# Seven extra weight tiles instead of four, expert rows gathered from x, and first units multiplied kind by kind in a two-block fp32 kernel on one core

## The chip, the cores and the metric

The kernel runs on one core of a Trainium2 chip as a single launch. The metric is device time in microseconds (us), here the median of three runs of the kernel before: 1743.42 us (1740.96 to 1744.84). All inputs and weights are fp32 in HBM and have to be fetched once: the trace counts 548 MB, of which the experts of two mixture layers are 403 MB.

## The reference, cut to what matters

One sequence of 256 tokens with 1024 features goes through a first block of two layers and then a second block. What the change touches, in the reference's own functions:

```
def modulate(x, g, shift, scale):                 # before every mixer and every expert layer
    return rmsnorm(x, g) * (1 + scale) + shift

def ec_moe(h, w_router, w_gate, w_up, w_down):    # 16 experts, each takes its best 32 tokens
    cap = 2 * n // 16
    aff = softmax(h @ w_router);  g, idx = top_k(aff.swapaxes(1, 2), cap)
    xs = h[idx]
    a = silu(xs @ w_gate) * (xs @ w_up)
    y = (a @ w_down) * g;  return zeros.at[idx].add(y)

layer 0:  x += g_m * even_mixer(modulate(x));  x += g_f * ec_moe(modulate(x))   # attention and Fourier
layer 1:  x += g_m * odd_mixer(modulate(x));   x += g_f * ec_moe(modulate(x))   # gated short convolution
second_block: mLSTM and attention in parallel, cross attention to mem, then relu^2 feed-forward
```

A row's RMS factor is a scalar per token. It can therefore be applied to the row, to the one-hot matrix that picks the row, or inside the matrix that transposes it; the result is the same up to rounding.

## The kernel before

Everything is written by hand: five engine programs (TensorE, VectorE, ScalarE, GpSimd, SyncE) joined by semaphores, with no scheduler. The order of each engine's instructions is the order of its Python code, and an engine that waits holds up everything behind it.

**The ring.** Weights come in units of 1 MB (128 partitions x 2048 fp32), listed by `weight_units` and issued in that order by SyncE alone. They go to `ring`, 12 slots (`SLOTS`); outside the expert layers only 8 of these (`TAIL`) are in the rotation, since the other 4 hold the two parts, `hi` and `lo`, of units that are multiplied in split form. `room(g)` in SyncE's program waits until the unit that sat in the slot has been read.

**An expert layer.** An expert has 12 units: 4 of gate, 4 of up, 4 of down. `pe_moe` computes router logits (`lgp`, `lgn`), VectorE makes softmax, top 32 and the one-hot matrices `take_p` (tokens x places), and `expert(e)` then runs 16 times: gather 32 rows by one-hot matmul (L727), transpose, gate and up (L742), silu and product, down (L765), and scatter into four PSUM banks (L774). After each unit TensorE raises `MOE_READ`, which lets SyncE refill the slot. The first two experts are unrolled. Expert 0's units fill the 12 ring slots; the first 4 units of expert 1 go to `extra` tiles, 1 MB stretches of SBUF that are idle just then (scratch at 42, 0 and 8 KB, and `hT`). So 16 units can be there when expert 0 begins; `left` and `turn_of` name for each extra tile what SyncE waits for and where in its order the load stands.

**Rows for the experts.** ScalarE squares x, VectorE makes the factor, and both scale x into `xn` (`norm_rows`, `scaled`); the gather reads `xn`.

**Split products.** The layer-1 mixer (`CONV_ORDER`, 16 units), the attention input (`in0`) and the feed-forward (`FF_ORDER`) multiply fp32 as three fp32r products: hi x hi, hi x lo, lo x hi. ScalarE casts a unit to `hi` (`round_weights`, L2015), VectorE subtracts to `lo` (`rest_of_weights`, L1466), and the three products are taken together for each k (L636, L651, L530), so the first product of a stage waits for both parts of both operands.

**The joints.** From layer 0's experts to the mixer: add the four banks to x, squares, factor, scale rows to `xn`, 16 transposes (L495), scale and shift (`turned`), cast and subtract for the rows, then unit 0. From layer 1's experts to the second block: VectorE first norms the rows of `mem` (L1224) and only then adds the banks to x (L1437), after which x is transposed (L503) for `in2.0` (L544).

## Time and profile before

| | |
|---|---|
| median of 3 runs | 1743.42 us (1740.96 to 1744.84) |
| the profiled execution, its own time | 1744.17 us |
| its span, first to last instruction | 1742.3 us |
| mean granted TensorE clock | 0.877 of full |
| TensorE busy | 1347.6 us, 77% |
| VectorE, ScalarE busy | 545.5 us, 348.4 us |
| moved by DMA | 548.10 MB, mean 315 GB/s |

The profiled execution lies 0.75 us above the median, and 1.9 us of it are outside the span. The page's 40 slices are 43.6 us each. Two long stretches at 421 to 422 GB/s are the expert layers (slices 8 to 16 and 21 to 30); between and behind them the traffic is much lower and TensorE is near fully busy. An instruction's line (L742) is its line in the kernel. A timeline row gives start, length, engine, line, tiles and count, and in brackets how long the engine had been idle and who released it; consecutive rows of one group are merged, so a length can span several instructions. An fp32 matmul has two records in the trace, a transpose or an fp32r product has one.

### The profile page before, as it was taken

The numbers are of one execution on the slowest core, as the hardware profiler recorded it, in microseconds if no ns is written. First come the engines' busy times: TensorE is split into PE (matmuls) and PEld (weight loads), VectorE is DVE, ScalarE is ACT, GpSimd is POOL, SyncE is SP. The second block draws the span as 40 slices with busy tenths as digits, with TensorE's granted clock in tenths as the row PEclk, the third lists the DMA queues.
The fourth block names the chain that finished last, engine by engine and source line by source line (L and its number), as shares of the span: only waits on it lengthen the run. The fifth ranks groups of instructions, "written<-read, shape, count | busy, mean of one in ns | idle before, by whom it ended". The sixth has DMA issues, their size and how long they took to land. (4 is left out here: it accounts for less than half of the span.)

```text
span 1742.3 us, 29625 instructions
## 1 busy us (share of the span) xinstructions
PE 1347.6 (77%) x12416; PEld 903.6 (52%) x12416; DVE 545.5 (31%) x1168; ACT 348.4 (20%) x610; POOL 27.9 (2%) x54
## 2 busy tenths in 40 slices
PE   3999996765665667599676667667668979989998
PEld 1997583322222223299442233233337856778997
DVE  2576753101010100256411010000103266555554
ACT  2413421000000000243300000000002132254443
POOL 2010100000000000000000000000000000000000
PEclk8999997889789887899798787887879997999999
DMA  9986898999999999965699999999998420345550
GB/s 329 361 293 236 282 361 345 420 422 421 422 422 422 422 421 421 389 210 172 269 420 421 422 422 421 422 422 422 422 421 265 139 85 12 114 150 176 192 167 25
DMA packets 145053, 548.10 MB, mean 315 GB/s; under 512 B 9630, under 2 KB 77632, under 8 KB 95704
## 3 DMA queue, kind: packets, MB, share of 16 engines
q1 hardware_dynamic: 142336, 542.18, 79.3%
q10 hardware_dynamic: 1080, 4.16, 0.7%
q0 software_dynamic: 1568, 0.77, 0.4%
q8 instruction: 51, 0.84, 0.2%
q14 instruction: 18, 0.15, 0.0%
HBM read 546.03 MB, written 1.05 MB: 314 GB/s over the span
## 5 line engine op out<-in xcount | busy, mean ns | idle before, releaser
L742 PE MATMUL bank<-ring,scratch 128*32 128x256 f32 x3968 | 311.4, 462 | 161.5 <-DMA ring<-in_moe_w_up 112.4
L742 PEld LDWEIGHTS bank<-ring,scratch 128*32 128x32 f32 x3968 | 134.7, 127 | 322.6 <-DMA ring<-in_moe_w_up 173.4
L765 PE MATMUL bank<-ring,scratch 128*32 128x256 f32 x2048 | 161.5, 463 | 60.7 <-DMA ring<-in_moe_w_down 44.8
L636 PE MATMUL bank<-scratch_split,ring_split 128*128 128x256 f32 x1344 | 161.2, 281 | 7.8 <-DVE scratch_split L1584 5.8
L636 PEld LDWEIGHTS bank<-scratch_split,ring_split 128*128 128x128 f32 x1344 | 160.1, 192 | 9.6 <-issue 6.0
L1418 DVE COPY scratch<-bank 128x256 f32<-128x256 f32 x32 | 13.6, 424 | 452.1 <-PE bank L751 452.1
L765 PEld LDWEIGHTS bank<-ring,scratch 128*32 128x32 f32 x2048 | 68.3, 130 | 147.2 <-DMA ring<-in_moe_w_down 74.2
L1466 DVE TENSOR_TENSOR ring_split<-ring,ring_split 128x2048 fp32r<-128x2048 f32 x48 | 110.0, 2292 | 76.8 <-ACT ring_split L2015 76.7
L516 PE MATMUL bank<-ring,hT 128*128 128x256 f32 (+1 forms) x512 | 112.8, 381 | 1.3 <-DVE hT L1233 0.7
L1997 ACT ACTIVATE scratch<-bank 128x256 f32<-128x256 f32 x32 | 12.3, 384 | 503.7 <-PE bank L742 503.7
L516 PEld LDWEIGHTS bank<-ring,hT 128*128 128x128 f32 x512 | 97.2, 193 | 14.6 <-issue 2.1
L2015 ACT CAST ring_split<-ring 128x2048 fp32r<-128x2048 f32 x48 | 91.3, 1904 | 57.3 <-PE bank L1145 36.8
L530 PE MATMUL bank<-ring_split 128*128 128x256 f32 x512 | 94.3, 288 | 9.2 <-DVE ring_split L1458 9.2
L1145 PE MATMUL bank<-ring_split,scratch_split 128*128 128x512 f32 x384 | 90.7, 392 | 0.5 <-DVE scratch_split L1897 0.5
L1425 DVE TENSOR_TENSOR scratch<-bank,gate 128x256 f32<-128x256 f32 x32 | 13.6, 424 | 245.7 <-PE bank L765 245.7
L530 PEld LDWEIGHTS bank<-ring_split 128*128 128x128 f32 x512 | 80.0, 193 | 12.0 <-DVE ring_split L1458 9.6
L1145 PEld LDWEIGHTS bank<-ring_split,scratch_split 128*128 128x128 f32 x384 | 70.9, 188 | 15.5 <-issue 1.1
L1993 ACT COPY scratch<-bank 128x256 f32<-128x256 f32 x32 | 11.9, 373 | 305.9 <-PE bank L727 305.9
L559 PE MATMUL bank<-ring,cond 128*32 128x256 f32 x768 | 50.9, 403 | 14.5 <-DMA ring<-in_ada_w 14.5
L774 PE MATMUL bank<-scratch 32*128 32x256 f32 x512 | 42.2, 447 | 20.4 <-DVE scratch L1425 20.4
L1397 DVE TENSOR_TENSOR scratch<-bank,gain 128x128 f32<-128x128 f32 x64 | 15.6, 286 | 106.0 <-PE bank L732 106.0
L774 PEld LDWEIGHTS bank<-scratch 32*128 32x128 f32 x512 | 27.7, 206 | 36.1 <-issue 35.7
(418 smaller groups left out, 1416.2 us busy)
## 6 DMA issues: line engine op xcount, KB each, us to landing
ring<-in_moe_w_up SPq DMA_DIRECT2D x128, 1024.0 KB, 26.7
ring<-in_moe_w_down SPq DMA_DIRECT2D x128, 1024.0 KB, 26.5
ring<-in_moe_w_gate SPq DMA_DIRECT2D x120, 1024.0 KB, 25.4
ring<-in_ada_w SPq DMA_DIRECT2D x48, 1024.0 KB, 8.8
ring<-in_w_ff SPq DMA_DIRECT2D x32, 1024.0 KB, 5.3
ring<-in_conv_w_in SPq DMA_DIRECT2D x12, 1024.0 KB, 11.9
ring<-in_attn_w_in SPq DMA_DIRECT2D x10, 1024.0 KB, 11.8
ring<-in_w_in SPq DMA_DIRECT2D x7, 1024.0 KB, 11.9
```

Of the source, the lines that this page charges most:

```text
L516: mm = nc.tensor.matmul(T[:, t * 256:t * 256 + width], lhs[:, k, t * P:(t + 1) * P], W[:, k, :], start=(k == ks[0]), stop=(k == ks[-1]))
L530: mm = nc.tensor.matmul(T[:, t * 256:t * 256 + 256], ht[:, k, t * P:(t + 1) * P], wt[:, k, :], start=(k + i == 0), stop=(k == KD - 1 and i ...
L559: mm = nc.tensor.matmul(T[32 * j:32 * j + 32, c0:c0 + 256], cond[:, k, :], W[:, a, j * 256:j * 256 + 256], start=(k == 0), stop=(k == 7))
L636: mm = nc.tensor.matmul(T[:, m * SEQ:(m + 1) * SEQ], wt[:, k, m * P:(m + 1) * P], ht[:, k, :], start=(k + i == 0), stop=(k == KD - 1 and i ...
L742: mm = nc.tensor.matmul(GU[32 * j:32 * j + 32, m * 256:(m + 1) * 256], xs[:, k % 2, 16 * k - k % 2 * 16:16 * k - k % 2 * 16 + 32], W[:, (k ...
L765: mm = nc.tensor.matmul(Y[32 * g:32 * g + 32, 0:256], actT[:, b, 32 * j:32 * j + 32], W[:, b * D + g * 256:b * D + (g + 1) * 256], start=( ...
L774: mm = nc.tensor.matmul(banks[4 + g][:, t * 256:(t + 1) * 256], comb[32 * g:32 * g + 32, t * P:(t + 1) * P], y_s[32 * g:32 * g + 32, :], s ...
L1145: mm = nc.tensor.matmul(acc[2 * t + c][:, :], ht[:, u % 2, a, t * P:(t + 1) * P], wt[:, a, c * 512:(c + 1) * 512], start=(u + a + i == 0), ...
L1397: ins = V.tensor_tensor(own, T[:, b * P:(b + 1) * P].rearrange("p (g c) -> p g c", g=4), bc(gain[:, l, 2, b::2].unsqueeze(2), [P, 4, CAP]) ...
L1418: V.tensor_copy(comb, banks[1][:, 256:512]).then_inc(comb_ready, 1)
L1466: give("w_split", V.tensor_tensor(lo[n % 2], ring[:, q, :], hi[n % 2], ALU.subtract))
L2015: sig("w_hi").give(A.copy(w_parts[p][0][n % 2], ring[:, q, :]))
```

## The change

- `EXTRA` = 7 extra tiles take the first 7 units of expert 1, and `TURN` = 5 is now the number of ring slots whose refill belongs to expert 1. The new tiles are `table_tile` (the constants that aren't needed then), `rows_tile` (`xn`) and `upper` (scratch at 34 KB). The constant table is put in another order for it, small buffers of the expert layer move, and `mask_q` is loaded a second time behind `mem`.
- The gather reads x itself. The row factor (`row_scale`) is multiplied into `take_p`, and `aff` is multiplied by its inverse so that the scatter weights stay as they were.
- The layer-1 rows are transposed by a matmul with `diag`, the identity times the row factor, in place of scaled rows and transposes; ScalarE writes the `hi` part straight from PSUM. `pe_gate(1, 2)` moves from the joint to behind the fourth conv unit.
- The first unit of each split stage (`pe_in0_first`, `pe_split_first`) is multiplied kind by kind: all hi x hi, then the weights' lo, then the rows' lo.
- At the start SyncE no longer waits for two small loads, and unit `in0.0` is cast before the rows. The norm of `mem` moves behind the rotary angles. The output is stored in four parts of 256 KB.

```diff
-for _name, _n in (("ident", 128), ("rank", CAP), ("cos", 128), ("sin", 128), ...
+for _name, _n in (("ident", 128), ("rank", CAP), ("inv_freq", 32), ("fold", 16), ("spread", 128), ("mask_k", 512),
+                  ("pick", 512), ("pick_ada", 512), ("mask_q", 512), ("dft_cos", 512), ("dft_sin", 512),
+                  ("grp_cos", 128), ("grp_nsin", 128), ("cos", 128), ("sin", 128)):
...
-        extra = [[high, low, turned_tile, mid], [high, mid, low, turned_tile]]
+        turned_tile, rows_tile = carve(HT, 0, UNIT), carve(XN, 0, UNIT)
+        table_tile = carve(TB, TABLE["mask_q"][0] / 256.0, UNIT)
+        extra = [[table_tile, high, low, turned_tile, rows_tile, mid, upper],
+                 [table_tile, high, upper, mid, low, rows_tile, turned_tile]]
...
-        base = [(TAIL + TAIL * l) % SLOTS for l in range(3)]
+        base = [(TAIL + TURN * l) % SLOTS for l in range(3)]
...
-            if isinstance(e, int) and e == 1 and s < 4:
+            if isinstance(e, int) and e == 1 and s < EXTRA:
                 return extra[l][s], extra_landed[s], 16 * (l + 1)
-            i = s if isinstance(e, int) and e == 0 else (s + TAIL) % SLOTS
+            i = s if isinstance(e, int) and e == 0 else (s + TURN) % SLOTS
...
+        def pe_split_first(pe, p, name, h, bank):
+            ...
+            sig("w_hi").take(pe, (1, len(CONV_ORDER))[p])
+            for b in range(4):
+                sig(("h1_hi", "h4_hi")[p]).take(pe)
+                run(hi, h[0], (2 * b, 2 * b + 1), first=True)
+            pe_split_unit(pe, p, 0)
+            run(lo, h[0], range(KD))
+            for b in range(4):
+                sig(("h_split", "h4_split")[p]).take(pe)
+                mm = run(hi, h[1], (2 * b, 2 * b + 1), last=True)
...
-                                              xn[:, t, g * 256:(g + 1) * 256], start=(t == 0), stop=(t == 1))
+                                              x[:, t, g * 256:(g + 1) * 256], start=(t == 0), stop=(t == 1))
...
-            pe_gate(pe, 1, 2)
             pe_ada_cols(pe, 1, 1)
-            pe_turn_rows_after(pe, "n1")
+            sig("diag_ready").take(pe)
+            for b in range(4):
+                T = tile(pe, f"n1.{b}")
+                for i in range(4):
+                    k = 2 * b + i // 2
+                    mm = nc.tensor.matmul(T[:, i * P:(i + 1) * P], x[:, i % 2, k * P:(k + 1) * P], diag[:, i % 2, :],
+                                          start=True, stop=True)
+                done(f"n1.{b}", mm)
             for n, (part, u) in enumerate(CONV_ORDER):
                 if n == 4:
+                    pe_gate(pe, 1, 2)
                     pe_router_bias(pe, 1)
...
+                        step(ins)
+                    own = take_p[:, :, e:e + n, :].rearrange("p t e c -> p t (e c)")
+                    return V.tensor_tensor(own, own, bc(row_scale.unsqueeze(2), [P, 2, n * CAP]), ALU.mult)
...
-                if l == 1:
-                    v.wait_ge(loads["mem"], 16)
-                    norm_rows(mem_raw, mem_n, ss_ctx)
-
                 for b in range(4):
                     v.wait_ge(combined, 4 * (e0 + NEXP - 1) + b + 1)
...
-            norm_rows(x, xn, ss, 2)
+            sig("squares_ready").take(v)
+            step(V.tensor_reduce(ss[:, 0:2], pieces[:, :, 0:2], AX, ALU.add))
+            rms(ss, [(0, 2, D)])
+            for t in range(TT):
+                ins = V.tensor_scalar(diag[:, t, :], ident, ss[:, t:t + 1], None, ALU.mult)
+            give("diag_ready", ins)
...
+            v.wait_ge(loads["mem"], 16)
+            norm_rows(mem_raw, mem_n, ss_ctx)
             T = product(v, "rbc")
...
+            round_in0(0)
             sig("gain_ready").take(s)
             turned("nx", hT, modulation(0, 0), (1, 3))
             rounded_rows("nx", hT, x_hi)
-            round_in0(0)
...
-            sp.wait_ge(loads["cond"], 32)
-            sp.wait_ge(loads["ident"], 16)
...
-                    turn_of = ({4: (0, 1), 8: (2,), SLOTS: (3,)}, {TAIL: (0,), SLOTS: (1, 2, 3)})[l]
+                    left = (("ao11", "ao11", "o0T.2", "out0.3", "squares", "lgp0", "lgp0"),
+                            (None, "conv_b.3", "conv_b.3", "out1.3", "out1.3", "squares", "lgp1"))[l]
+                    turn_of = ({4: (0, 1, 2), 8: (3,), SLOTS: (4, 5, 6)}, {0: (0,), TAIL: (1, 2), SLOTS: (3, 4, 5, 6)})[l]
...
+                        at = TABLE["mask_q"][0]
+                        sp.dma_start(table[:, at:at + 512], w["constants"][:, at:at + 512]).then_inc(loads["mask"], 16)
...
-            sp.wait_ge(sig("out_ready").sem, 4)
-            sp.dma_start(out[0].rearrange("(t p) d -> p t d", p=P), x[:, :, :]).then_inc(stored, 16)
+            for b in range(4):
+                t, cols = b // 2, slice((b % 2) * 512, (b % 2) * 512 + 512)
+                sp.wait_ge(sig("out_ready").sem, b + 1)
+                sp.dma_start(out[0, t * P:(t + 1) * P, cols], x[:, t, cols]).then_inc(stored, 16)
...
+EXTRA = 7
+TURN = SLOTS - EXTRA
```

How the change moves instructions is seen at three places. First SyncE's order at layer 0's expert layer: the loads of expert 0 (gate, up, down, in `ring`) and of expert 1 (in `scratch`, `hT`, `table`, `xn`), up to the first refills. Before:

```order
L2376 DMA ring<-in_moe_w_gate 128x2048 x4
L2376 DMA scratch<-in_moe_w_gate 128x2048 x2
L2376 DMA ring<-in_moe_w_up 128x2048 x4
L2376 DMA hT<-in_moe_w_gate 128x2048
L2376 DMA ring<-in_moe_w_down 128x2048 x4
L2376 DMA scratch<-in_moe_w_gate 128x2048
L2376 DMA ring<-in_moe_w_up 128x2048 x4
L2376 DMA ring<-in_moe_w_down 128x2048 x4
```

and in the changed kernel:

```order
L2462 DMA ring<-in_moe_w_gate 128x2048 x4
L2462 DMA table<-in_moe_w_gate 128x2048
L2462 DMA scratch<-in_moe_w_gate 128x2048 x2
L2462 DMA ring<-in_moe_w_up 128x2048 x4
L2462 DMA hT<-in_moe_w_gate 128x2048
L2462 DMA ring<-in_moe_w_down 128x2048 x4
L2462 DMA xn<-in_moe_w_up 128x2048
L2462 DMA scratch<-in_moe_w_up 128x2048 x2
L2462 DMA ring<-in_moe_w_up 128x2048
L2462 DMA ring<-in_moe_w_down 128x2048 x4
```

Three loads stand ahead of the first refill that were behind it: one to the table, issued with the first gate units, and two at the end. Second, TensorE's order in the joint from layer 0's experts (L774 is their last matmul, L828 in the changed kernel) to the layer-1 mixer. Before:

```order
L774 MATMUL bank<-scratch 128x256 x8
L583 MATMUL bank<-scratch,table 128x256 x4
L575 MATMUL bank<-table,scratch 128x128 x4
L495 MATMUL bank<-table,xn 128x128 x16
L636 MATMUL bank<-scratch_split,ring_split 128x256 x192
L662 MATMUL bank<-router,ada_col 128x16 x8
```

and in the changed kernel:

```order
L828 MATMUL bank<-scratch 128x256 x8
L605 MATMUL bank<-table,scratch 128x128 x4
L994 MATMUL bank<-scratch,x 128x128 x16
L665 MATMUL bank<-scratch_split,ring_split 128x256 x48
L692 MATMUL bank<-scratch_split,ring_split 128x256 x144
L613 MATMUL bank<-scratch,table 128x256 x4
L718 MATMUL bank<-router,ada_col 128x16 x8
```

The gate matmuls (L583, now L613) have gone from the joint to behind the fourth unit, and 16 matmuls from x with `diag` stand where 16 transposes were. Third, VectorE's order at the entry of the second block. Before:

```order
L1206 TENSOR_SCALAR st<-st 128x2
L1212 RECIPROCAL st<-st 128x2
L1224 TENSOR_SCALAR ring<-ring,st 128x1024
L1437 TENSOR_TENSOR x<-x,bank 128x2x256 x4
L1233 TENSOR_SCALAR hT<-bank,vec 128x256 x4
```

and in the changed kernel, with the last rows of the rotary angles:

```order
L1497 TENSOR_TENSOR x<-x,bank 128x2x256 x4
L1293 TENSOR_SCALAR hT<-bank,vec 128x256 x4
L1696 TENSOR_REDUCE st<-st 128x2
...
L1714 MEMSET scratch 128x8
L1266 TENSOR_SCALAR st<-st 128x2
L1272 RECIPROCAL st<-st 128x2
L1284 TENSOR_SCALAR ring<-ring,st 128x1024
L1718 COPY scratch<-bank 128x256
```

The three instructions that norm `mem` (the tile in `ring`) no longer stand ahead of the addition of the experts' result to x.

## Rows read from the trace of the kernel before

**Rows 1.** The page: GB/s in each of 40 slices.

```profile
GB/s 329 361 293 236 282 361 345 420 422 421 422 422 422 422 421 421 389 210 172 269 420 421 422 422 421 422 422 422 422 421 265 139 85 12 114 150 176 192 167 25
```

**Rows 2.** Stretches: length, busy us PE, PEld, DVE, ACT, POOL, clock, DMA share, GB/s.

```profile
306.00:722.00 416.00, 271.65 (x3280) 120.03 (x3272) 39.45 (x170) 18.06 (x46) 0.00 (x0) 0.84 1.01 422
...
248.00:258.00 10.00, 10.00 (x72) 8.01 (x74) 2.77 (x4) 1.49 (x6) 0.00 (x0) 1.00 0.59 199
274.00:286.00 12.00, 9.49 (x98) 4.31 (x102) 4.57 (x15) 0.37 (x1) 0.00 (x0) 0.57 0.42 152
...
860.00:868.00 8.00, 6.30 (x58) 2.66 (x54) 3.46 (x12) 0.37 (x1) 0.00 (x0) 0.50 0.14 39
```

**Rows 3.** Timeline of SyncE's loads around the first experts of both layers.

```profile
262.95 0.33 SPq L2376 DMA_DIRECT2D scratch<-in_moe_w_gate  x1
281.13 4.65 SPq L2376 DMA_DIRECT2D ring<-in_moe_w_up  x4
304.15 2.92 SPq L2376 DMA_DIRECT2D ring<-in_moe_w_up  x4
318.86 4.59 SPq L2376 DMA_DIRECT2D ring<-in_moe_w_gate  x4
...
848.07 0.33 SPq L2376 DMA_DIRECT2D hT<-in_moe_w_gate  x1
```

**Rows 4.** Timeline of VectorE ahead of expert 0: the one-hot matrices.

```profile
274.27 1.80 DVE L1374 TENSOR_TENSOR scratch<-scratch,table 128x64 f32<-128x64 f32 x4
```

**Rows 5.** Timeline of the joint from layer 0's experts to the mixer.

```profile
727.72 1.99 PE L583 MATMUL bank<-scratch,table 128*128 128x256 f32 x8 [0.73 <-DVE x L1437]
...
731.75 0.17 DVE L1212 RECIPROCAL st<-st 128x2 f32<-128x2 f32 x1 [0.34 <-ACT st L1956]
...
735.02 2.29 DVE L1466 TENSOR_TENSOR ring_split<-ring,ring_split 128x2048 fp32r<-128x2048 f32 x1 [1.84 <-ACT ring_split L2015]
736.02 1.02 ACT L1968 ACTIVATE hT<-bank,ada_col,gain 128x256 f32<-128x256 f32 x2
...
748.71 0.59 ACT L2155 COPY scratch<-bank 128x512 f32<-128x512 f32 x1 [5.42 <-PE bank L636]
```

**Rows 6.** Timeline of TensorE: the mixer's first units, and a later gap.

```profile
740.98 19.25 PE L636 MATMUL bank<-scratch_split,ring_split 128*128 128x256 f32 x150 [5.84 <-DVE scratch_split L1584]
...
802.44 12.79 PE L636 MATMUL bank<-scratch_split,ring_split 128*128 128x256 f32 x96 [1.74 <-DVE ring_split L1466]
```

**Rows 7.** Groups by form: fp32 matmuls of 128 columns; busy, mean ns.

```profile
L606 PE MATMUL bank<-ring,scratch 128*128 128x128 f32 x32 | 5.9, 311 | 0.0
```

**Rows 8.** Timeline of the joint from layer 1's experts to the second block.

```profile
1310.00 1.15 PE L774 MATMUL bank<-scratch 32*128 32x256 f32 x16 [0.65 <-DVE scratch L1425]
...
1315.54 2.48 DVE L1437 TENSOR_TENSOR x<-x,bank 128x512 f32<-128x512 f32 x4
...
1319.75 8.22 PE L544 MATMUL bank<-hT,ring 128*128 128x256 f32 x32
...
1328.26 7.07 PE L544 MATMUL bank<-hT,ring 128*128 128x256 f32 x32
```

**Rows 9.** Two stretches in which TensorE's granted clock changes or holds.

```profile
726.00:739.00 13.00, 5.39 (x44) 0.98 1.10 350
...
1315.00:1323.00 8.00, 6.71 (x26) 0.57 1.10 348
```

**Rows 10.** Timeline of the start.

```profile
3.72 18.46 SPq L2414 DMA_DIRECT2D ring<-in_ada_w  x8
...
48.48 1.91 ACT L2048 CAST ring_split<-ring 128x2048 fp32r<-128x2048 f32 x1 [7.45 <-DMA ring<-in_attn_w_in]
...
51.79 1.93 PE L559 MATMUL bank<-ring,cond 128*32 128x256 f32 x32
```

**Rows 11.** Timeline of TensorE: the feed-forward's first unit, second part.

```profile
1562.19 9.12 PE L636 MATMUL bank<-scratch_split,ring_split 128*128 128x256 f32 x78 [0.19 <-DVE st L1877]
```

**Rows 12.** Transfers: KB each, median us from issue to landing.

```profile
out<-x SPq DMA_DIRECT2D x1, 1024.0 KB, 4.0
```

156 lines of the change are left out of this document (103 added, 53 removed).

## The prediction, made before the changed kernel was run

> **What bounds the kernel now.** I read the traffic by slices first [rows 1]: two plateaus at 421 to 422 GB/s, each one expert layer, and much less elsewhere. The reader is to see that the kernel has two kinds of stretches. In the plateaus DMA ends last: from 306 to 722 us it moves 422 GB/s while TensorE is busy 272 of 416 us [rows 2]. A unit of 1.049 MB takes 1.049/422 = 2.485 us there, an expert of 12 units 29.8 us. TensorE alone needs far less: SyncE's refills follow its reads, and from the refill at the 17th read, 304.15, to that at the 25th, 318.86, pass 14.7 us for 8 reads and a change of expert [rows 3]; 12 reads come to about 18 us. Outside the plateaus TensorE or the chain of small steps at a joint ends last. So a layer ends at the time of its first refill plus the units that are then still to be moved. It comes earlier by more units moved before that, or by an earlier first refill; nothing inside the 16 experts counts.
>
> I then read the stretches around the first experts for idle DMA [rows 2]. From 248 to 258 us it moves 199 GB/s, which is 10 x (1 - 199/422) = 5.3 us idle; from 274 to 286 us 152 GB/s, 7.7 us idle; in layer 1 from 860 to 868 us 39 GB/s, 7.3 us idle, and more in the mixer before. SyncE has issued its last extra load by 262.95 and 848.07 and has no tile left until the first read, 281.13 in layer 0 [rows 3]. Last I read the three joints and the start in the timeline.
>
> **Layer 0, three more tiles.** Worth 3 x 2.485 = 7.46 us if all three move in idle time and the queue doesn't run dry afterwards. The table tile is issued next to the first gate units and pushes 2.5 us of work into the gap of 5.3. The other two are released by the squares and by the logits, near 262.95 where the fourth extra load goes out now; they need 4.97 us and the gap behind has 7.7. All 19 units are there before the first read. Afterwards 12 refills follow expert 0's reads, 5 of expert 1 and 7 of expert 2, and the next needs the 20th read, about 307 us (304.15 + 2.92). The 12 keep DMA busy from about 282 to 312, so it has 5 us to spare. The refill at the 25th read, 318.86, meets a queue that ends at 282.3 + 17 x 2.485 = 324.6. No bubble, 7.46 us. Against it stands VectorE's extra product into `take_p` for the first two experts, 128 elements a row: the four comparisons take 1.80 us in all [rows 4], so I take 0.3 us with the step. The wait for `xn` that goes was over long before. Term: 7.15 us, bounds 4.7 (only two tiles count) and 7.5.
>
> **Joint from layer 0 to the mixer.** Now the factor is ready at 731.92, the first unit starts at 740.98 and its result is copied at 748.71 [rows 5, 6]. In the changed kernel, by the same durations: diag by 732.4; 16 fp32 matmuls of 128 columns, 32 records, at most 5.9 us by the nearest row [rows 7], so done by 738.3. ScalarE casts the unit from 731.7 to 733.6 (1.91 us, as in [rows 10]) and writes 8 hi chunks at 0.51 us [rows 5] to 737.8, each after its n1 bank, in the worst case to 739.3. VectorE's 2.29 us [rows 5] for the unit end near 736, its share of the rows near 738, four subtractions near 740.9. TensorE does hi x hi behind n1, then the other 32 products, and ends unit 0 near 743 to 745.5, against 748.6 now. But unit 1 waits for ScalarE's cast behind its last hT chunks (to 742) and VectorE's 2.29 us: 744.4. It starts 4.2 us earlier than now, and often behind a gap of 1 to 2 us on TensorE. The nearest row for that is the gap of 1.74 us at 802.44 [rows 6]: the 96 products behind it take 12.79 us, and by 9.12 us for 78 [rows 11] they would take 11.1 at the full clock. So I charge 1.7 us. The gate matmuls, 1.99 us [rows 5], are now hidden, since TensorE waits for the rows; behind the fourth unit TensorE is the bound, so 1.7 us (all but the first one's latency) are paid in full. ScalarE's two gate copies there are hidden by the router bias and a unit of 5.5 us. Term: 4.2 - 1.7 - 1.7 = 0.8 us, bounds -1.0 and 2.6.
>
> **Layer 1, three more tiles.** 7.46 us again. One is issued ahead of all and one with the high tile, both into the idle time of the mixer [rows 1], so only one unit more is in the tail. The last load now goes out at 848.07 [rows 3] and the gap opens at 860 [rows 2]; that unit takes 2.5 of its 7.3 us. -0.3 for `take_p`, +0.15 since ScalarE loads its exp table sooner (layer 1 waits for it, layer 0 doesn't). Term: 7.3 us, bounds 4.8 and 7.6.
>
> **Joint from layer 1 to the second block.** The last expert matmul starts at 1310.00; x is updated from 1315.54 [rows 8], since VectorE norms `mem` first. Without that it starts when those matmuls end, 1311.15: 4.4 us. Then in2.0, now 1319.75 to 1327.8, runs partly at the low clock: 0.57 from 1315 to 1323 us [rows 9]. In the changed kernel TensorE idles under 1 us, until the first addition of 0.62 us is done, in place of 5.0, so the clock should hold. Then in2.0 takes 6.9 us like its successor (7.07 [rows 8] with the first one's latency) in place of 8.1. It also starts sooner behind the additions: they take 2.48 us and the last transposes about 0.6, so 3.1 us in place of 4.2 (1319.75 - 1315.54). Together 2.3 us. The repeated `mask_q` load puts 0.25 MB, 0.7 us, ahead of in2.0's weights, which land about when they are needed: -0.2. The `mem` norm, moved, has 6 us until its transposes. Term: 6.5 us, bounds 4.4 and 6.9.
>
> One rule of the Trainium skill speaks against the clock part. The page TensorE: Matmul & The Clock Gate, section Part 4: PE-mode transpose, says that transposes don't count as TensorE being busy. By that rule the transposes at this joint wouldn't hold the clock, in2.0 would start at full speed and lose it on the way, and the term would be rival C's 4.7. The trace doesn't decide it: from 726 to 739 us the clock is 0.98 with 5.4 us of work, transposes among it [rows 9], and no row has transposes alone ahead of a fall.
>
> **Start.** SyncE's first load goes out at 3.72 [rows 10], held by two small loads; now nothing stands ahead of it, about 3 us. In part of that time x is already being fetched, so I give the stream half, 1.5 us. The cast of in0.0 before the rows and the order by kind let unit in0.0 end about 5 us sooner, but in0.1 waits for DMA: its cast is at 48.48, its lo part done at 52.8, and TensorE takes it at 53.7, behind 1.93 us of ada matmuls from 51.79 [rows 10]. So the gain is 1.5 + 0.9 and perhaps 0.6 since `ctx` is issued later, 3.0 us, less what a 3 us gap ahead of in0.1 costs in clock, up to 2.5. Term: 1.5 us, bounds -0.5 and 3.5.
>
> **Feed-forward and output.** The first ff1 unit now waits for the last rows' lo part, at 1562.19, with 30 of 48 products behind it [rows 11]; by kind only 16 come behind it, and 0.45 us remain after the hi chunks' own timing; bounds 0 and 1. The output of 1 MB takes 4.0 us from issue to landing [rows 12]; the last quarter moves 0.79 MB less, 1.9 us, and I take 1.7; bounds 0.5 and 1.9. By the fixed cost that the Trainium skill gives (DMA: Bandwidth & Descriptors, Anatomy of one DMA), about 2.0 us, an estimate for the last quarter is 2.6 us and the gain 1.4.
>
> **Sum.** 7.15 + 0.8 + 7.3 + 6.5 + 1.5 + 0.45 + 1.7 = 25.4 us. The profiled execution took 1744.17 (span 1742.3, 1.9 outside it), so 1718.8; the median of the three runs lies 0.75 below it, so 1718.0 us.
>
> **Rivals.** (A) The tiles bring less: the queue runs dry or the late loads come after the first read, each layer gains 2.5 us in place of 7.3. For it: SyncE works in strict order, and two loads hang on ScalarE's squares; against it: the 5 us to spare worked out above. 25.4 - 9.6 = 15.8, time 1727.6. (B) The clock never falls: no loss at the mixer's unit 1 (1.7) nor at in0.1 (1.5), 1714.8. For it: 0.98 over 13 us of sparse work [rows 9]; against it: the gap at 802.44 [rows 6]. (C) The clock does fall at the second block's entry: in2.0 keeps its 8.1 us and half the sooner start goes, so 6.5 becomes 4.7 and the time 1719.8. The rule of the Trainium skill named above would bring this about. For it: the fall near 1315, TensorE having last done ordinary matmuls at 1311; against it: the idle time that went with it. (D) Slower: a bubble in every lap of the ring. SyncE refills in the order of reads, and the ring is seated anew (expert e's unit s now at slot s+5). If the slot freed first weren't the one wanted next, DMA would idle once per expert. There are about 14 laps behind the unrolled experts in each layer, 28 in all, so it decides from 25.4/28 = 0.9 us per lap; at 1.2 us the time is 1718.0 + 33.6 = 1751.6. Against it: a slot is reused after 12 units as before, with 11 loads (27 us) outstanding. (E) The change doesn't do what it says, the loads being in flight but all held by one earlier wait: only joints, start and end count, 10.95 us, 1732.5.
>
> **Chances.** Forecast 0.5, B 0.13, C 0.17, A 0.1, E 0.05, D 0.03, and 0.02 for no change by several losses. About 0.2% (3.5 us) is what a measurement of this kernel can tell. Faster by more than that 0.95, within 0.02, slower 0.03. B and C lie within the forecast's own range, 1713 to 1724; A reaches to 1728, and the sum of the low bounds is 12.9 us, 1730.5, that of the high ones 31.5, 1711.9. I give 1711 to 1729.
>
> **What would show it.** GB/s of 422 from the first read on, with under 3 us idle between 274 and 286 us; expert layer 0 ending 7 to 11 us earlier than now; unit 0 of the mixer by 743 to 745.5 minus that shift, and unit 1 behind a gap; from the last expert matmul of layer 1 to the end of in2.0 11.3 us in place of 17.8; the last store landing about 2.3 us after its issue. Wrong would be: a plateau below 420 GB/s, experts more than 29.9 us apart, or DMA idle between reads 12 and 25 of either layer.

## The result and the profile after

The changed kernel takes 1717.5 us (median of 4 runs, 1715.6 to 1724.0) against 1743.8 us before (4 runs beside them, 1741.0 to 1744.8): a ratio of 0.9863, 95% interval 0.9842 to 0.9884. The prediction was 1718.0 us, 1711 to 1729. The profiled execution took 1716.49 us, its span 1714.7 us, 27.6 us shorter than the span of before. TensorE's mean granted clock is 0.877 of full, as before.

Cutting both spans at the same instructions shows where the 27.6 us come from. The cuts are SyncE's first load of `attn_w_out`, the last scatter of each expert layer (L774 before, L828 after), the first refill of a ring slot in layer 1, SyncE's loads of `w_ukv`, `w_out` and the first of `w_ff`, and the end. The third column gives the range over all other traces of the study that run the same code there, with their number in brackets; it matters, since it is wide in some stretches. The kernel before has one trace. In the fifth row the values fall into two groups.

```
stretch, us                                before    after   same code, other runs
start, to load of attn_w_out               204.56   205.24   203.0 to 204.5 (7)
to last scatter of layer 0                 521.29   513.44   512.4 to 513.5 (8)
to first refill of layer 1                 140.02   138.21   138.5 to 141.9 (6)
to last scatter of layer 1                 444.13   436.83   436.0 to 437.6 (8)
to load of w_ukv                            34.01    27.78   27.7 to 27.8 (6), 29.6 to 30.0 (4)
to load of w_out                            27.63    27.63   27.6
to first load of w_ff                      129.72   126.37   124.3 to 132.2 (8)
to the end                                 240.94   239.20   238.7 to 240.9 (7)
```

The traffic by slices, as in [rows 1], on the page after:

```profile
GB/s 342 340 293 258 258 391 375 420 422 422 421 422 422 422 422 422 398 231 197 319 404 421 422 422 422 422 422 422 422 422 316 141 86 13 123 147 178 193 171 25
```

Both plateaus have the same height and are shorter; the slice ahead of the first has risen from 345 to 375 GB/s, those ahead of the second from 172 and 269 to 197 and 319. That is where the new tiles are loaded. The stretches of [rows 2] after the change (columns as there):

```profile
248.00:258.00 10.00, 10.00 (x60) 8.20 (x62) 2.29 (x4) 1.38 (x5) 0.00 (x0) 1.00 0.81 324
274.00:286.00 12.00, 9.04 (x104) 4.29 (x108) 6.16 (x18) 0.37 (x1) 0.00 (x0) 0.62 0.85 330
306.00:700.00 394.00, 270.61 (x3176) 122.56 (x3172) 38.78 (x168) 15.80 (x42) 0.00 (x0) 0.81 1.01 422
```

From 274 to 286 us DMA is idle for 12 x (1 - 330/422) = 2.6 us in place of 7.7 (what is missing from the plateau's 422 GB/s, counted as idle time). SyncE's loads around it, as in [rows 3], and the first refill of layer 1:

```profile
262.54 0.43 SPq L2462 DMA_DIRECT2D xn<-in_moe_w_up  x1
263.64 0.81 SPq L2462 DMA_DIRECT2D scratch<-in_moe_w_up  x2
281.95 0.33 SPq L2462 DMA_DIRECT2D ring<-in_moe_w_up  x1
...
856.89 0.33 SPq L2462 DMA_DIRECT2D ring<-in_moe_w_up  x1
```

The late tiles go out from 262.54 to 264.45, 17 to 19 us ahead of the first refill. The start, against [rows 10] (timelines of SyncE, ScalarE and TensorE, and a stretch):

```profile
0.75 1.46 SPq L2506 DMA_DIRECT2D ring<-in_ada_w  x3
...
47.14 1.90 ACT L2123 CAST ring_split<-ring 128x2048 fp32r<-128x2048 f32 x1 [9.81 <-DMA ring<-in_attn_w_in]
...
8.64 0.28 PE L857 MATMUL bank<-table,scratch 16*128 16x16 f32 x1 [8.64 <-DMA table<-in_constants]
...
44.22 1.93 PE L589 MATMUL bank<-ring,cond 128*32 128x256 f32 x32
51.60 0.77 PE L560 MATMUL bank<-ring_split 128*128 128x256 f32 x2 [5.45 <-DVE ring_split L1518]
```
```profile
54.00:70.00 16.00, 16.00 (x143) 14.71 (x145) 7.29 (x8) 6.95 (x8) 0.00 (x0) 0.88 1.05 386
```

SyncE's first load is 2.97 us sooner, the cast of `in0.1` only 1.34 us. Unit `in0.0` and the ada products (L589) are done at 46.15, and TensorE then idles 5.45 us; its clock from 54 to 70 us is 0.88, where it was 1.00. So `in0.1` starts at 51.60, 2.05 us sooner than before (53.65), but its 48 products take 8.66 us in place of 5.93. The joint to the mixer, TensorE (against [rows 5, 6]):

```profile
718.68 1.15 PE L828 MATMUL bank<-scratch 32*128 32x256 f32 x16 [0.64 <-DVE scratch L1489]
720.65 0.72 PE L605 MATMUL bank<-table,scratch 128*128 128x128 f32 x4 [0.82 <-DVE x L1497]
725.32 6.13 PE L994 MATMUL bank<-scratch,x 128*128 128x128 f32 x32 [3.96 <-DVE scratch L1641]
731.21 5.90 PE L665 MATMUL bank<-scratch_split,ring_split 128*128 128x256 f32 x48
738.92 7.34 PE L692 MATMUL bank<-scratch_split,ring_split 128*128 128x256 f32 x48 [1.81 <-DVE ring_split L1526]
...
758.71 1.85 PE L718 MATMUL bank<-router,ada_col 128*128 128x16 f32 x16
```

The last row, the first router products, is the first instruction behind the new place of the gate matmuls that both kernels have. It comes 40.0 us behind the last scatter (718.68); in the kernel before it was 39.0 us (725.85 to 764.83). Up to there the joint is longer than before, not shorter.

And its entry to the second block (against [rows 8]):

```profile
1293.72 1.15 PE L828 MATMUL bank<-scratch 32*128 32x256 f32 x16 [0.64 <-DVE scratch L1489]
1295.60 2.45 PE L507 MATMUL bank<-table,x 128*128 128x128 f32 x16 [0.73 <-DVE x L1497]
1298.29 7.17 PE L574 MATMUL bank<-hT,ring 128*128 128x256 f32 x32 [0.24 <-DMA ring<-in_w_in]
1305.30 0.61 PE L1021 MATMUL bank<-table,st 128*128 128x128 f32 x4
```

From the last scatter to the end of `in2.0` pass 1305.30 - 1293.72 = 11.6 us, against 17.8.

### The profile page after: what moved, and what is told of

Read it like the earlier page. It is cut to its first block and busy times, and to the rows that moved or that the text cites. A ratio compares the mean times of both kernels' runs of the same rounds, so it can differ in the third digit from the quotient of the medians.

```text
span 1714.7 us, 29683 instructions
## 1 busy us (share of the span) xinstructions
PE 1346.7 (79%) x12432; PEld 907.1 (53%) x12432; DVE 547.6 (32%) x1175; ACT 347.0 (20%) x613; POOL 27.9 (2%) x54
## 3 DMA queue, kind: packets, MB, share of 16 engines
HBM read 546.29 MB, written 1.05 MB: 319 GB/s over the span
## 5 line engine op out<-in xcount | busy, mean ns | idle before, releaser
L692 PE MATMUL bank<-scratch_split,ring_split 128*128 128x256 f32 x1248 | 148.4, 280 | 3.6 <-DVE ring_split L1526 3.6
L692 PEld LDWEIGHTS bank<-scratch_split,ring_split 128*128 128x128 f32 x1248 | 147.5, 190 | 5.1 <-DVE ring_split L1526 4.0
L560 PE MATMUL bank<-ring_split 128*128 128x256 f32 x480 | 88.8, 289 | 5.5 <-DVE ring_split L1518 5.5
L560 PEld LDWEIGHTS bank<-ring_split 128*128 128x128 f32 x480 | 75.4, 194 | 8.0 <-issue 8.0
L2073 ACT COPY scratch<-bank 128x256 f32<-128x256 f32 x32 | 11.9, 372 | 289.4 <-PE bank L781 289.4
L828 PE MATMUL bank<-scratch 32*128 32x256 f32 x512 | 41.4, 440 | 20.5 <-DVE scratch L1489 20.5
L589 PE MATMUL bank<-ring,cond 128*32 128x256 f32 x768 | 49.6, 398 | 6.4 <-DMA ring<-in_ada_w 4.8
L828 PEld LDWEIGHTS bank<-scratch 32*128 32x128 f32 x512 | 27.4, 200 | 35.1 <-issue 34.9
## 6 DMA issues: line engine op xcount, KB each, us to landing
ring<-in_conv_w_in SPq DMA_DIRECT2D x12, 1024.0 KB, 11.9
```

The source lines that it names most:

```text
L560: mm = nc.tensor.matmul(T[:, t * 256:t * 256 + 256], ht[:, k, t * P:(t + 1) * P], wt[:, k, :], start=(k + i == 0), stop=(k == KD - 1 and i ...
L589: mm = nc.tensor.matmul(T[32 * j:32 * j + 32, c0:c0 + 256], cond[:, k, :], W[:, a, j * 256:j * 256 + 256], start=(k == 0), stop=(k == 7))
L692: mm = nc.tensor.matmul(T[:, m * SEQ:(m + 1) * SEQ], wt[:, k, m * P:(m + 1) * P], ht[:, k, :], start=(k + i == 0), stop=(k == KD - 1 and i ...
L828: mm = nc.tensor.matmul(banks[4 + g][:, t * 256:(t + 1) * 256], comb[32 * g:32 * g + 32, t * P:(t + 1) * P], y_s[32 * g:32 * g + 32, :], s ...
```

## The experiments

Each is the changed kernel with one edit (the last three with several, the second block's with one at each of its waits), run beside the kernel before on the same chip. Ratios are to the kernel before; stretches are those of the table. Single executions of the kernel before lie between 1734.1 and 1747.5 us, and the intervals of the ratios reach 3.6 to 8 us to either side. So a verdict on one step rests on its stretch, read in one trace of each kernel.

**Four tiles in place of seven.**

```
-EXTRA = 7
+EXTRA = 4
-extra = [[table_tile, high, low, turned_tile, rows_tile, mid, upper], ...
+extra = [[high, low, turned_tile, mid], [high, mid, low, turned_tile]]
```

The lists `left` and `turn_of` are shortened to match.

> The changed kernel with four extra tiles per layer in place of seven (rows still gathered from x, all joints as changed). Theory of the sum: three units of 2.485 us per layer come back into the tail, 7.3 + 7.3 us more than the changed kernel's 1717.5, so 1732.1 us. Rival A (the late tiles bring 2.5 us a layer, the rest of the gain is in the joints): 1722.5 us.

Measured: 1729.0 us, ratio 0.9932 (0.9903 to 0.9961), 12 us worse than seven tiles by the ratios. Layer 0 takes 519.97 us, 7.0 more than the mean of 513.0 over nine traces with seven; layer 1 takes 443.58, 6.8 more than their mean of 436.8. So three units are worth 6.8 to 7.0 us per layer out of the 7.46 that they take to move. Rival A, with 2.5 per layer, is out.

**SyncE's two waits at the start put back.**

```
+            sp.wait_ge(loads["cond"], 32)
+            sp.wait_ge(loads["ident"], 16)
             for item in units:
```

> The changed kernel with SyncE's two waits at the start put back (its first weight load waits for the small loads of cond and ident). In the changed kernel the first load goes out at 0.75 us in place of 3.72, but cond lands 5 us later and the first ada matmul comes only 1 us sooner; the cast of in0.1 came 1.3 us sooner. Theory S1: that 1.3 us is what the removed waits gave, so 1718.8 us. Rival S2: the wait only exchanged one delay for another, 1717.5 within 0.4.

Measured: 1720.7 us, 0.9871 (0.9831 to 0.9910), too wide to tell the two apart. Its stretch is 205.88 us, against 203.0 to 205.2 in the eight traces without the waits (mean 203.8): 2.1 us. Its cast of `in0.1` is at 48.06, 0.9 later. `in0.1` starts at 52.52, 1.4 later than the mean of 51.2 in the eight traces, which is S1's 1.3; the rest is its length, 8.40 us against a mean of 7.66, and that alone varies from 7.2 to 8.7 with the same code. S1 has the right sign; one trace doesn't settle the size. What the removed waits cost stands in the list of transfers (KB each, us from issue to landing), before and then after; the first two rows of each are x and `ident`:

```profile
x<-in_x ACTq DMA_DIRECT2D x1, 1024.0 KB, 6.0
table<-in_constants ACTq DMA_DIRECT2D x1, 64.0 KB, 1.9
```
```profile
x<-in_x ACTq DMA_DIRECT2D x1, 1024.0 KB, 11.7
...
table<-in_constants ACTq DMA_DIRECT2D x1, 64.0 KB, 6.9
```

With 3 MB of weights in flight the small loads land 5 us later, and TensorE's first instruction (L857) with them.

**The norm of `mem` back ahead of the additions.** In `moe` on VectorE (shown) and ScalarE, whose squares of `mem` move with it:

```
+                if l == 1:
+                    v.wait_ge(loads["mem"], 16)
+                    norm_rows(mem_raw, mem_n, ss_ctx)
                 for b in range(4):
                     v.wait_ge(combined, ...)
```

> The changed kernel with the norm of mem put back ahead of the additions of layer 1. Theory of the sum: the additions start 4.4 us later and TensorE's clock falls in the gap, 1.3 to 2.3 us more: 5.7 to 6.7 us slower than the changed kernel, 1723.7 us, and the granted clock under 0.8 over the first 10 us after the gap. Rival (clock does not depend on that gap): 4.4 us, 1721.9 us with the clock at 1.00. Rival (norm of mem is no longer hidden where it stands now, so putting it back costs little): 1719 us.

Measured: 1722.8 us, 0.9878 (0.9833 to 0.9924), an interval too wide for a step of 6 us. TensorE, and the clock of a stretch with it and of the changed kernel's own:

```profile
1294.80 1.15 PE L828 MATMUL bank<-scratch 32*128 32x256 f32 x16 [0.65 <-DVE scratch L1489]
1301.03 3.68 PE L507 MATMUL bank<-table,x 128*128 128x128 f32 x16 [5.08 <-DVE x L1500]
1304.49 8.28 PE L574 MATMUL bank<-hT,ring 128*128 128x256 f32 x32
```
```profile
1300.00:1308.00 8.00, 6.97 (x27) 6.39 (x28) 5.41 (x15) 5.93 (x16) 0.00 (x0) 0.57 1.10 348
```
```profile
1297.00:1305.00 8.00, 7.76 (x39) 6.57 (x38) 5.50 (x24) 5.81 (x16) 0.00 (x0) 1.00 1.10 348
```

The way to the `w_ukv` load is 34.02 us, 6.24 more than 27.78 and what the kernel before has. Of it 4.35 us are the longer wait (5.08 in place of 0.73). The other 1.9 lie in the same instructions at a clock of 0.57 in place of 1.00: `in2.0` starts 3.46 us behind the first transpose in place of 2.69, and takes 8.28 in place of 7.17.

**The second units by kind too.** `in0.1` and `conv_c.1` take the 32 products with the high half of the weights first, and the 16 with the low half behind VectorE's subtraction:

```
+            if name == "in0.1":
+                sig("in0_hi").take(pe)
+                run(h[0], hi, first=True)
+                run(h[1], hi)
+                sig("in0_split").take(pe)
+                mm = run(h[0], lo, last=True)
...
+            if n == 1 and p == 0:                 # the same with w_hi and w_split
```

> The changed kernel with the second unit of the start (in0.1) and the second unit of the mixer (conv_c.1) multiplied kind by kind too: the 32 products that need only the high half first, the 16 with the low half behind VectorE's subtraction. Theory G (the gaps of 5.45 us ahead of in0.1 and 1.81 us ahead of conv_c.1 are on the path, with the low clock behind them): both units start 2.4 and 1.8 us sooner, and the mixer's one at the full clock, 1.5 us more: 5.5 us faster than the changed kernel, 1712 us. Rival (DMA sets the pace of both stretches, 383 and 349 GB/s): within 1 us of 1717.5.

Measured: 1712.5 us, 0.9824 (0.9785 to 0.9863). `in0.1` on TensorE:

```profile
48.52 2.73 PE L558 MATMUL bank<-ring_split 128*128 128x256 f32 x16 [2.94 <-ACT ring_split L2158]
51.05 3.02 PE L558 MATMUL bank<-ring_split,hT_split 128*128 128x256 f32 x16
53.91 2.08 PE L558 MATMUL bank<-ring_split 128*128 128x256 f32 x16
```

The start takes 200.94 us (in four traces with this edit 200.7 to 201.3), 2.9 us less than the mean of 203.8. The stretch from layer 0's end to the first refill of layer 1 takes 135.82, 3.9 less than the mean of the seven traces without a change there (139.7). Up to the first router products it is 36.9 us (714.18 to 751.10) against a mean of 39.8, so 2.9 of the 3.9 lie where the edit stands; the rest lies in a part that varies with the same code, as the next run shows. Theory G's 5.5 us came as 2.9 and 2.9, and DMA doesn't set the pace of either.

**The gate matmuls back in the joint**, ahead of `diag`, with ScalarE's two copies ahead of its `n1` work:

```
+            pe_gate(pe, 1, 2)
             pe_ada_cols(pe, 1, 1)
             sig("diag_ready").take(pe)
...
                 if n == 4:
-                    pe_gate(pe, 1, 2)
```

> The changed kernel with the gate matmuls of the mixer and ScalarE's two gate copies put back into the joint behind layer 0, ahead of the rows. Sum theory (prediction: moving them behind the fourth unit costs 1.7 us of TensorE time there and saves nothing in the joint, where TensorE waits for the factor anyway): in the joint TensorE waits 3.96 us for the factor and the gate matmuls take 1.9 to 2.0, so putting them back saves 1.7 us: from the last scatter of layer 0 to the first refill of layer 1 136.7 us in place of 138.2 to 140.3. Rival (ScalarE's two gate copies, 0.5 us each, stand ahead of its work for n1 and delay the first unit): 138 to 139.5 us, no gain.

Measured: 1714.6 us, 0.9830 (0.9803 to 0.9858), and 134.30 us for the stretch: 5.4 less than the mean of 139.7, 3.9 less than the changed kernel's own trace. The joint on TensorE:

```profile
716.26 1.68 PE L828 MATMUL bank<-scratch 32*128 32x256 f32 x16 [0.64 <-DVE scratch L1489]
718.63 3.78 PE L613 MATMUL bank<-scratch,table 128*128 128x256 f32 x8 [0.68 <-DVE x L1497]
722.21 1.06 PE L605 MATMUL bank<-table,scratch 128*128 128x128 f32 x4
723.39 3.91 PE L995 MATMUL bank<-scratch,x 128*128 128x128 f32 x32
...
752.09 1.85 PE L718 MATMUL bank<-router,ada_col 128*128 128x16 f32 x16
```

The first router products come 35.8 us behind the last scatter, where seven traces without the edit have 38.7 to 40.5 (mean 39.8, the changed kernel's own 40.0): 4.0 us, more than the sum theory's 1.7. Behind them the same code takes 98.2 to 101.4 us from one execution to the next, and this trace has a short case, 98.5; so the 5.4 us are too much, and 4.0 it is. Of these, 1.7 are the gate matmuls that no longer stand behind the fourth unit (L613 to L718 in the changed kernel, 756.98 to 758.71). The other 2.3 are clock and an earlier second unit. The rows product, 6.13 us in the changed kernel, takes 3.91 here (the changed kernel's window first, then two of this one):

```profile
725.00:731.00 6.00, 5.68 (x30) 5.68 (x31) 4.67 (x10) 3.72 (x6) 0.00 (x0) 0.57 1.10 350
```
```profile
716.00:723.00 7.00, 6.05 (x28) 4.41 (x28) 3.24 (x9) 3.21 (x10) 0.00 (x0) 0.55 1.10 350
723.00:727.00 4.00, 3.88 (x33) 3.61 (x32) 3.23 (x7) 3.94 (x7) 0.00 (x0) 0.93 1.10 349
```

In this trace the low clock lies on the gate matmuls, which take 3.78 us in place of 1.99 and still end before the factor is ready; without them TensorE idles 3.96 us, and the low clock lies on the rows. But here the clock had fallen before the gates began: the 16 scatter records take 1.68 us in place of 1.15. Two later traces with the gates and no extra products in the joint, below, have the gates at the full clock (1.99 us) and rows of 5.47 us. A gain up to the router products is there again, 2.4 us against the same kernel without them; that the gates shield the rows is one trace's case, not a rule.

**The output stored whole again.** One transfer behind the last quarter:

```
-            for b in range(4): ... sp.dma_start(out[0, t * P:(t + 1) * P, cols], x[:, t, cols])
+            sp.wait_ge(sig("out_ready").sem, 4)
+            sp.dma_start(out[0].rearrange("(t p) d -> p t d", p=P), x[:, :, :])
```

> The changed kernel with the output stored by one transfer behind the last quarter, as before. Prediction: 1.7 us later from the last issue to the end of the span (4.0 in place of 2.3 us). Rival (a store costs mostly a fixed time): under 0.7 us.

One run, 1722.9 us, so only its trace counts. VectorE's last additions of this kernel and of the changed one:

```profile
1713.50 3.11 DVE L1980 SCALAR_TENSOR_TENSOR x<-bank,st,x 128x512 f32<-128x512 f32 x4 [3.94 <-PE bank L1205]
```
```profile
1709.09 3.11 DVE L1980 SCALAR_TENSOR_TENSOR x<-bank,st,x 128x512 f32<-128x512 f32 x4 [3.94 <-PE bank L1205]
```

They end at 1716.61 and 1712.20, the spans at 1721.1 and 1714.7: 4.5 us behind in one, 2.5 in the other. Storing in quarters is worth 2.0 us; 1.7 was expected.

**Idle TensorE time at the expert layers' entries filled.** Products of `ident` with `ident` into a bank that is overwritten, 0.28 us each at the full clock; they compute nothing that is used.

```
             T = tile(pe, f"ord{l}", bank=1)
+            warm(T, 20)
             sig("order_ready").take(pe)
...
+            warm(banks[3], 5)
             sig("take_ready").take(pe)
```

> The changed kernel with idle TensorE time at the entry of both expert layers filled: 20 products of ident with ident ahead of the wait for the order, 5 ahead of the wait for take_p, into banks that are overwritten. In the changed kernel the granted clock is 0.62 to 0.75 there and DMA moves only 252 and 326 GB/s in the first 8 us behind the first refill, since the reads come too slowly. Theory (the clock of the first reads is on the path of a layer): gather, transposes and the first read run at the full clock, first refill 1.5 us sooner, and the first 8 reads faster: 2 to 3 us per layer, 1712.5 us. Rival (the layer's end hangs on DMA alone): 0.5 us or less per layer, 1717 us.

Measured: 1716.5 us, 0.9854 (0.9825 to 0.9882). The first 16 us around the first refill, in the changed kernel and with the products:

```profile
275.00:291.00 16.00, 12.37 (x157) 5.90 (x161) 6.50 (x18) 1.13 (x3) 0.00 (x0) 0.75 0.87 329
```
```profile
274.00:290.00 16.00, 12.86 (x194) 7.80 (x196) 6.90 (x20) 1.13 (x3) 0.00 (x0) 1.00 0.93 370
```

From the last router products to the last scatter it takes 453.7 us in place of 455.7 in layer 0, and 453.8 in place of 455.2 in layer 1: 3.4 us in all, between the theory (4 to 6) and its rival (1); by the means of the nine traces without the products (455.2 and 455.8) it is 3.4 too. The median, 1716.5, can't show it. The gain wasn't found again: in the run of everything together, with 18 and 4 products at the same places, the same two stretches take 455.4 and 454.6 us, which is 0.9 us less than the means, and in layer 0 the clock fell behind the products all the same (the first 128 records of L842 take 8.53 us, 7.11 here). So 3.4 us is one trace's gain.

**Idle TensorE time in the second block filled.**

```
+                if i == 0:
+                    warm(T, 12)
                     copied(pe, "ckvT")
...
+                    warm(T, 16)
                     for k in range(4):
                         sig("uc_ready").take(pe)
...
+                        warm(T, 18)
                         sig("qk_ready").take(pe)
...
+                if i < 2:
+                    warm(T, (5, 8)[i])
                 sig(f"{name}_exp").take(pe)
```

> The changed kernel with idle TensorE time in the second block filled with products of ident with ident into banks that are overwritten: 12 ahead of ukv, 16 ahead of qm, 18 ahead of the turned q and k, 5 and 8 ahead of the first two exponentials of the second attention. In all traces so far the stretch from the first in_wo_x load to the first in_w_ff load takes either 66.5 us (clock low for some 9 us) or 71.1 to 71.4 us (low for some 23 us) with the same code, and the stretch before it 32.8 to 35.7. Theory (the falls of the clock behind TensorE's waits make these stretches long and uneven): with the waits filled the clock stays at 1.00 there and the stretch takes 61 to 63 us; from the in_w_out load to the in_w_ff load 120 in place of 126.4 to 132.2 us; 1709 us in all. Rival (the chain of ScalarE and VectorE steps ends last there, the clock only changes how TensorE waits): within 2 us of 1717.5.

Measured: 1715.4 us, 0.9839 (0.9816 to 0.9863). The clock is 0.98 from 1407 to 1476 us, but from the first `wo_x` load to the first `w_ff` load 68.65 us pass, and 241.8 to the end behind it. Of the forecast nothing came: the 18 products stood at a wait of 0.72 us, and the first scores came 28.9 us behind the `wo_x` load in place of 25.5. These 3.4 us hide what the other products gave: behind the scores it is 39.8 us to the `w_ff` load, 41.1 in the changed kernel.

**The same, each filling no longer than its wait.** The 18 are gone, 4 stand ahead of `gcol` and 14 ahead of the turned `hm`:

```
-                    warm(T, 12)        # ukv
+                    warm(T, 10)
-                    warm(T, 16)        # qm
+                    warm(T, 12)
-                        warm(T, 18)
                         sig("qk_ready").take(pe)
...
+                    warm(T, 14)
                     sig("hm_ready").take(pe)
...
-                    warm(T, (5, 8)[i])
+                    warm(T, (3, 4)[i] if name == "b" else (3, 0)[i])
```

> The changed kernel with the waits of the second block filled again, now by the length of each wait (0.28 us per product, as the last run showed): 4 ahead of gcol (1.2 us), 10 ahead of ukv (3.15), 12 ahead of qm (3.95), 14 ahead of the turned hm (4.44), 3 and 4 ahead of the first exponentials of the second attention, 3 in the third. The last run had 18 products in front of a wait of 0.72 us and came to the second attention 3.4 us later after the first in_wo_x load (28.9 in place of 25.5). Theory (the clock falls behind these waits are on the path, and only products that don't outlast a wait are free): clock 1.00 from the in_w_out load to the in_w_ff load, which takes 119 to 121 us in place of 124.3 to 132.2, and 1709 us in all. Rival (the chain of ScalarE and VectorE is what ends last): 124 us or more, though the clock is 1.00.

Measured: 1711.6 us, 0.9821 (0.9797 to 0.9845). From the `w_out` load to the first `w_ff` load 122.44 us in place of 124.3 to 132.2. The last stretch of it here, in the changed kernel, and in the kernel with the second units by kind (same code there, a long case):

```profile
1407.00:1472.00 65.00, 56.53 (x304) 46.88 (x303) 45.80 (x112) 21.08 (x58) 0.00 (x0) 0.97 0.11 33
```
```profile
1409.00:1475.00 66.00, 55.58 (x265) 45.18 (x266) 45.82 (x112) 21.62 (x58) 0.00 (x0) 0.90 0.10 33
```
```profile
1404.00:1475.00 71.00, 62.58 (x270) 50.29 (x271) 45.89 (x113) 21.32 (x58) 0.00 (x0) 0.81 0.10 30
```

The gain is there: 6.9 us less than the mean of nine traces (129.3), 1.9 less than the shortest, and the two later runs with the same products have 122.4 and 123.3. It is short of the 119 to 121 expected. Behind the products TensorE still waits 1.31 us for VectorE's `hm` and 0.66 to 1.30 for ScalarE's exponentials, so the chain of the other two engines, which the rival named, has its share; how much wasn't measured.

**By kind and gates together, no extra products.** The edits of both runs:

```
+            if name == "in0.1":                   # by kind
+            if n == 1 and p == 0:                 # by kind
+            pe_gate(pe, 1, 2)                     # in the joint
```

> The changed kernel with in0.1 and conv_c.1 by kind and the gate matmuls back in the joint, no extra products. Theory: the two gains add where they have different causes. Start to the first in_attn_w_out load 200.9 us (as the run by kind) in place of 203.2 to 205.2; from the last scatter of layer 0 to the first refill of layer 1 the gates alone gave 134.3 and the kinds alone 135.8 in place of 138.2 to 140.3; together the unit's gap of 1.99 us goes too, at full clock: 132.3 to 133 us. Sum 3 + 5.5 us, 1709 us. Rival (both gave the same clock and nothing else): 134.3 us at the joint, 1711 us.

Measured: 1714.3 us, 0.9836 (0.9812 to 0.9861). The start is 201.34, as with the kinds alone; the joint's stretch is 134.92, as with the gates alone, which is what the rival said. The rows say otherwise:

```profile
713.99 1.15 PE L863 MATMUL bank<-scratch 32*128 32x256 f32 x16 [0.64 <-DVE scratch L1524]
715.87 1.99 PE L629 MATMUL bank<-scratch,table 128*128 128x256 f32 x8 [0.73 <-DVE x L1532]
...
720.63 5.47 PE L1030 MATMUL bank<-scratch,x 128*128 128x128 f32 x32 [2.31 <-DVE scratch L1676]
...
748.55 1.85 PE L753 MATMUL bank<-router,ada_col 128*128 128x16 f32 x16
```

From the scatter to the router products it is 34.6 us, 1.3 less than with the gates alone (35.8) and 2.4 less than with the kinds alone (36.9). Behind it this trace has 100.4 us where the gates' trace had 98.5, with the same code, and that hides it. So the two edits do add here, though not in full (4.0 and 2.9 alone, 5.3 together); the rival's single cause is not borne out. The median shows none of this.

**All of it together.** The two edits above, 18 and 4 products at the expert entries, and the second block as placed above:

```
+            warm(T, 18)
             sig("order_ready").take(pe)
...
+                    warm(banks[3], 4)
```

> The kernel of the two edits before it (by kind, gates back) with the extra products at both expert entries (18 and 4) and in the second block as placed in the first of these three runs. Theory: 1709 less 3 us at the entries (the earlier run with such products gave 1.4 to 2.0 per layer, from the last router products to the last scatter) and less 8 us in the second block: 1698 us. Rival (the second block's chain does not gain): 1705 us.

Measured: 1698.3 us (1694.0 to 1704.3, 5 runs), ratio 0.9742 (0.9720 to 0.9764). It beats the changed kernel, whose interval begins at 0.9842, by 1.2%. The second block repeats the 122.4 us of the run above. The end takes 237.2 (237.3 there), but the run below, with the same code at the end, has 240.9, so that isn't a gain of the products. The sum theory's 1698 is met. Not all of its terms are: the layers' entries gave 0.9 us in place of 3, and the profiled execution is the slowest of the five, 1704.3.

**Extra products inside the experts too.**

```
                             W, there_sem, count = expert_unit(l, e, 4 * m + k // 2)
+                            warm(banks[3], 2)
                             pe.wait_ge(there_sem, count)
```

> The kernel of all edits together with extra products inside the experts too: 2 (0.55 us) ahead of each of the 12 waits for a unit, of every expert, and 6 ahead of the wait for diag in the joint behind layer 0. In the traces the clock falls for some 8 us now and then in the experts, where TensorE waits 1.41 us for each unit, and where such a fall lies on the layer's end the way from there to the in_w_ukv load takes 29.6 to 30.0 us in place of 27.8. Theory: two products per wait keep the clock up over the layers and both exits: 27.8 us there, 131 us in place of 132.9 from the last scatter of layer 0 to the first refill of layer 1, the layers' pace unchanged at 422 GB/s, 1695 us in all. Rival 1: they are too few to hold the clock, or it falls at other places, 1698 us. Rival 2: with 6.6 us more work per expert TensorE falls behind DMA somewhere (full clock: 18 + 6.6 us of 29.8, at the low clock more than 29.8), 1702 us or more.

Measured: 1728.0 us, 0.9922 (0.9902 to 0.9943). The same 2 products stand ahead of the down units, and 6 ahead of `diag` in the joint. The exits are as the theory has them (27.3 us to the `w_ukv` load, 131.6 at the joint), but the layers are 11.9 and 13.7 us longer: rival 2. The same stretch of layer 0 without and with these products:

```profile
306.00:342.00 36.00, 26.04 (x404) 13.70 (x396) 4.78 (x22) 1.50 (x4) 0.00 (x0) 0.98 1.01 421
```
```profile
306.00:342.00 36.00, 32.36 (x391) 18.31 (x384) 2.77 (x12) 1.13 (x3) 0.00 (x0) 1.00 0.73 276
```

The reader is to see DMA fall to 276 GB/s, 12.5 us idle in 36: all of layer 0's loss. TensorE's second gather starts at 300.11 and its third at 327.12, so an expert takes 27.0 us, less than DMA's 29.8, and yet DMA starves. Expert 1's first seven reads are of extra tiles and free no slot, so the 12 refills behind expert 0 must last until the 20th read. The prediction gave that 5 us to spare, and in the changed kernel it holds: the 13th refill goes out at 306.47, 24.5 us behind the first, before the 12 x 2.485 = 29.8 us of the others are over. Here it goes out at 316.56, 38.4 us behind the first, and from 312 to 316 us DMA moves nothing.

## Why the prediction was right, step by step

- **Layer 0, three more tiles (7.15):** 7.0 against four tiles, 7.85 against before. Idle DMA of 2.6 us from 274 to 286, all 19 units out of the queue by the first refill, no bubble, 422 GB/s: as said. The extra product into `take_p` costs 0.3 us where it stands, as forecast: from the copy of the order to the first gather pass 1.09 us in place of 0.77. By the mean of nine traces the layer gained 8.3 against before, over the upper bound of 7.5. The 1.3 us between four tiles and the kernel before are not explained; runs of the same code differ by 1.
- **Joint to the mixer (0.8):** 1.8 in the profiled execution, 0.3 by the mean of seven traces, and both owe it to the part behind the router products, where the same code takes 98.2 to 101.4 us. Up to them the joint is 0.8 us longer by the mean (39.8 against 39.0), 1.05 in the changed kernel's own trace. The clock's charge of 1.7 came out (units 1 to 3 take 18.23 us, 16.61 at the full clock) and so did the 1.7 for the gates (1.73). The failed step is "It starts 4.2 us earlier than now": unit 1 starts 20.24 us behind the scatter in place of the 22.75 from which the forecast started, 2.5 earlier. The forecast let ScalarE's hi chunks end at 737.8, although by its own 5.9 us for the rows the later end, 739.3, holds; measured, in the time of before, they end at 739.7, and VectorE's part for unit 1 at 746.0 in place of 744.4. It also took the gates for mere length: leaving them in the joint gave 4.0 us and not 1.7.
- **Layer 1 (7.3):** 7.30; 6.8 against four tiles. The 0.15 for the exp table is measured by no run of its own.
- **Joint to the second block (6.5):** 6.23, and 6.24 when undone. 4.35 us of waiting and 1.9 of clock and what follows from it, against 4.4 and 2.3 less 0.2. That it came out so in the profiled execution is in part luck. Of twelve traces with this exit eight take 27.3 to 27.8 us and four take 29.6 to 30.0, close to rival C's 4.7. In those four the clock had fallen already in the last expert: the 16 scatter records take 2.09 us in place of 1.15. The wait at the joint is the same 0.7 us, so it isn't what brought the fall. What the prediction drew from the rule on transposes of the Trainium skill (TensorE: Matmul & The Clock Gate, Part 4: PE-mode transpose), that the clock would be lost on the way, would hold in all twelve. The eight, with the clock at 1.00 through 2.45 us of transposes and `in2.0`, don't bear that out here.
- **Start (1.5):** -0.7 in the profiled execution; the mean of eight traces, 203.8, makes it +0.8. The parts are the start and the length of `in0.1`. The forecast has it 3.0 us sooner and charges 1.5 for the clock; the mean is 2.5 sooner (51.2 against 53.65) and 1.7 longer (7.66 us against 5.93), the profiled execution 2.05 and 2.7. The stream gained 1.3, not 1.5, and the order by kind moved a wait instead of removing it: `in0.0` ended 7.6 us sooner, not 5, TensorE idled 5.45 us in place of the 3 foreseen, and `in0.1` ran its first 6 us at the low clock.
- **Feed-forward and output (0.45, 1.7):** from the last row's lo part to the copy of ff1's first unit it is 3.46 us in place of 3.93, so 0.47; the output 1.9 to 2.0. The estimate of 2.6 us worked out from the Trainium skill (DMA: Bandwidth & Descriptors, Anatomy of one DMA) was too high: the list of transfers has 2.1 us for a quarter. The page gives its figure for transfers issued by GpSimd; SyncE issues these.
- **Not in the sum:** 3.35 us between the `w_ukv` load and the first `w_ff` load, where no edit stands. It is a stretch that takes 152 to 160 us from one execution to the next. With it the profiled execution gained 27.6 us; the ratio stands for 23.9.
- **The other rivals:** A is out by the run with four tiles, B by the clock of 0.57 in the joint and 0.88 in the start, D by the 422 GB/s from 306 to 700 us, E by the layers' 7.85 and 7.30 us.

Taken stretch by stretch from the means over all traces with the same code, against the one trace of before, the gains are 0.8, 8.3, 0.3, 7.3, 5.6, 0 and 0.4, and 1.2 at the end: 23.9 us, which is also what the ratio gives. The forecast was 25.4. So it holds within its range, and the two large terms and the exit are shown by runs, but 1717.5 against 1718.0 is closer than a sum can be whose terms are off by up to 1.2 us both ways; that is luck. In the sum itself the high bounds add up to 31.0, not 31.5 (1712.4 us), which leaves the stated range as it is.
